# Second layer's input projection written out tile by tile, with its transposes inside it

## The reference, cut to what matters

```
p = x @ w_in                                   # 1024 -> 2888 columns
qc, kc, vc, qd, kd, vd, qi, ki, wi = split_cols(p, ODD_SPLIT)   # 512,512,512,512,128,128,512,64,8
new_rows = (kc, vc, kd, vd, ki)                # returned as caches, token by token
lam = exp(sum(lam_q1*lam_k1)) - exp(sum(lam_q2*lam_k2)) + lam_init
oc = diff_attention(qc, kc_all, vc_all, q_pos, lam, ...)
od = dsa_attention(qd, kd_all, vd_all, qi, ki_all, wi, q_pos)   # indexer picks 256 keys
mix = concatenate([oc, od]) @ w_out
x = layer_norm(ALPHA * x + mix, g1, b1)        # x is the residual
```

## Time and profile before

| | |
|---|---|
| median of 3 runs | 4275.34 us (4273.2 to 4279.86) |
| the profiled execution's own time | 4281.68 us |
| its span, first to last instruction | 4279.9 us |
| TensorE matmul busy | 3564.1 us (83%) |
| DVE busy | 2087.3 us (49%) |
| ACT busy | 910.1 us (21%) |
| mean granted TensorE clock | 0.891 of full speed |

### The profile page before, as it was taken

The page is one execution under the profiler, slowest core; times in us unless marked ns, Lnnn a source line. Parts: engine busy times, 40 slices in busy tenths (PEclk is TensorE's granted clock), DMA queues, the critical chain, the costliest instruction groups (busy, mean ns, idle before and its releaser), DMA issues. The chain is left out here.

```text
span 4279.9 us, 61244 instructions
## 1 busy us (share of the span) xinstructions
PE 3564.1 (83%) x26492; PEld 3237.0 (76%) x26492; DVE 2087.3 (49%) x2944; ACT 910.1 (21%) x1681; POOL 174.7 (4%) x75
## 2 busy tenths in 40 slices
PE   7977379858899999989967777777655989999997
PEld 7977169838899999979964445555434879999996
DVE  3115876565523232451125888988665452323235
ACT  1015311121201010120014444443223020101011
POOL 0010000002200000010020000000000220000001
PEclk9988589978999999989985788887677999999998
DMA  3110000011111111111120000001111111111111
GB/s 101 44 56 5 0 4 4 11 62 35 35 45 42 44 45 45 45 30 44 41 75 1 1 1 1 1 1 30 40 40 21 39 30 45 45 45 43 42 45 47
DMA packets 244527, 142.06 MB, mean 33 GB/s; under 512 B 36101, under 2 KB 237978, under 8 KB 243770
## 3 DMA queue, kind: packets, MB, share of 16 engines
q1 hardware_dynamic: 243320, 138.22, 11.2%
q10 hardware_dynamic: 962, 0.20, 0.0%
HBM read 123.14 MB, written 15.32 MB: 32 GB/s over the span
## 5 line engine op out<-in xcount | busy, mean ns | idle before, releaser
L238 PE MATMUL psum<-rounded,rounded 128*128 128x364 f32 x13536 | 2279.7, 330 | 96.6 <-DVE rounded L668 42.5
L238 PEld LDWEIGHTS psum<-rounded,rounded 128*128 128x128 f32 x13536 | 2270.6, 189 | 106.7 <-issue 81.7
L222 DVE CAST rounded<-arena 128x1024 fp32r<-128x1024 f32 x188 | 134.0, 713 | 401.5 <-PE psum L238 385.5
L541 ACT ACTIVATE arena<-psum 128x1092 f32<-128x1092 f32 x64 | 69.4, 1084 | 1213.7 <-PE psum L238 1213.7
L555 DVE CAST rounded<-arena 128x1092 fp32r<-128x1092 f32 x64 | 46.7, 729 | 533.1 <-ACT arena L544 533.1
L224 DVE TENSOR_TENSOR rounded<-arena,rounded 128x1024 fp32r<-128x1024 f32 x188 | 282.2, 1501 | 6.5
L2034 PE MATMUL psum<-arena 128*128 128x128 f32 (+2 forms) x1424 | 244.8, 327 | 42.2 <-ACT arena L2098 42.0
L1359 PE MATMUL psum<-arena 64*64 64x64 f32 x8160 | 256.7, 220 | 23.9 <-POOL arena L1543 12.5
L1359 PEld LDWEIGHTS psum<-arena 64*64 64x64 f32 x8160 | 246.1, 136 | 35.4 <-DVE arena L1496 18.4
L2034 PEld LDWEIGHTS psum<-arena 128*128 128x128 f32 (+1 forms) x1424 | 220.0, 235 | 67.6 <-issue 41.8
L2018 PE MATMUL psum<-arena 128*128 128x128 f32 (+1 forms) x712 | 143.2, 338 | 133.2 <-ACT arena L2089 132.6
(11 more groups left out here) (228 smaller groups left out, 2749.0 us busy)
## 6 DMA issues: line engine op xcount, KB each, us to landing
arena<-in_w_ff_up SPq DMA_DIRECT2D x128, 256.0 KB, 3.2
arena<-in_w_ff_down SPq DMA_DIRECT2D x128, 256.0 KB, 3.1
arena<-in_w_in_odd SPq DMA_DIRECT2D x46, 256.0 KB, 3.3
arena<-in_w_in_even SPq DMA_DIRECT2D x40, 256.0 KB, 3.3
x_kept<-arena SPq DMA_DIRECT2D x1, 4368.0 KB, 12.4
arena<-x_kept SPq DMA_DIRECT2D x1, 4368.0 KB, 13.1
arena<-in_x_prompt SPq DMA_DIRECT2D x1, 4096.0 KB, 18.7
arena<-in_cache_c_k SPq DMA_DIRECT2D x4, 1024.0 KB, 5.4
```

The lines of the kernel that those rows point to most:

```text
L222: nc.vector.tensor_copy(rounded(m, high), low).then_inc(self.weights_high, 1)
L238: last = nc.tensor.matmul(m.ps[:, out:out + TB], rounded(m, w)[:, k, :], rounded(m, x(k))[:, b * TB:(b + 1) * TB], start=(k == 0 and n == ...
```

## The change

`project_odd` is written out for every engine, with 23 tiles and no loop. The index keys and index weights share one tile (72 columns used), whose keys are copied to the other 64 partitions by a DMA. The order is: index keys, four tiles of C keys, D keys, four of C values, D values, then twelve of queries. While TensorE multiplies tile `u` it transposes tile `u - 2` (of the first eleven) in three groups, ahead of blocks k = 1, 4 and 7, into PSUM banks 3 and 7. DVE moves them out behind the next weight split. Keys go through two staging buffers, stored by SP when it has issued the load of the tile six later. Values are stored in two DMAs of all prompt rows each, and two for the sample.

The norm writes `x` to eight other tiles (`norm.dest`). SP writes them to DRAM (`x_kept`, 4368 KB) when all eight are made, and the setup block of `odd_attention` reads them back into `m.x` behind the three first constants and ahead of the distance table. `turn_rows` and its `join` are gone; lambda is computed in the new block, right behind the norm. Two attention buffers get their own room since `m.p` has 18 tiles instead of 24.

```
+ODD_TILES = ([("idx", 2816, 17)] + [("ck", 512 + 128 * a, 4 + a) for a in range(4)] + [("dk", 2048, 16)]
+             + [("cv", 1024 + 128 * a, 8 + a) for a in range(4)] + [("dv", 2176, 12)]
+             + [("cq", 128 * a, a) for a in range(4)] + [("iq", 2304 + 128 * a, 12 + a) for a in range(4)]
+             + [("dq", 64 * a, 8 + a) for a in range(4)])
 def project_odd(m, norm):
-    linear(m, "in1", 24, loads, 2, [(0, 1), (1, 3), (3, 4), (4, 5), (5, 6)], lambda k: m.x[:, k, :],
-           evacuate, norm=norm)
+    norm.dest = p[:, 8:16, :]
+    groups = [(0, 4), (4, 8), (8, 9)]
+    staged = [p[:, 14 + i, 0:512].rearrange("p (t c) -> p t c", t=4) for i in range(2)]
...
+        def _(sp):
...
+            for u in range(tiles):
+                ring.load(sp, 0, u, True, lambda slot: loads(u, slot))
+                if u == 3:
+                    sp.wait_ge(ring.x_high, ring.operands + 8)
+                    sp.dma_start(io["x_kept"], p[:, 8:16, :].rearrange("p k t -> p (k t)")).then_inc(kept, 16)
+                v = u - 6
+                if v in keys:
+                    store_rows(v)
+                if v == keys[0]:
+                    sp.wait_ge(turned, group_at(v, 2) + 1)
+                    sp.dma_start(p[64:128, 17, :], p[0:64, 17, :]).then_inc(doubled, 16)
+                if v == ODD_TURNED[-1]:
+                    sp.wait_ge(rows, group_at(v, 2) + 1)
+                    store_values("c_v", m.vn)
+                    store_values("d_v", m.vd)
...
+        def _(pe):
+            norm.tensor(pe)
+            def turn(u, g):
+                name, _, tile = ODD_TILES[u]
+                n = group_at(u, g)
+                if n >= 2:
+                    pe.wait_ge(rows, n - 1)
+                pe.wait_ge(ring.freed, ring.tiles + u + 1)
...
+            for u in range(tiles):
+                if u == 1:
+                    norm.scales_read(pe)
+                if u >= 2:
+                    pe.wait_ge(ring.freed, ring.tiles + u - 1)
+                def ready(k):
+                    if u == 0:
+                        pe.wait_ge(ring.x_split, ring.operands + k + 1)
+                    if u - 2 in ODD_TURNED and k in (1, 4, 7):
+                        turn(u - 2, k // 3)
+                ring.multiply(pe, 0, u, lambda k: high[:, k, :], lambda k: m.x[:, k, :], ready)
...
+        def _(act):
+            norm.scalar(act, ring, high)
+            act.wait_ge(lam_p, 2)
+            nc.scalar.activation(m.lam[:, 0:2], m.lam[:, 0:2], ACT.Exp).then_inc(lam_e, 1)
...
+        def _(dve):
+            norm.vector(dve, ring, high, lambda: ring.split(dve, 0, 0, 0, True))
+            def move(u, g):
...
+                    to = stores_before(u, g)
+                    if to >= 2:
+                        dve.wait_ge(stored[to % 2], 16 * (to // 2))
...
+            nc.vector.tensor_tensor(m.lam_in[:, 0:4:2, :], m.lam_in[:, 0:4:2, :], m.lam_in[:, 1:4:2, :], ALU.mult)\
+                .then_inc(lam_p, 1)
+            dve.wait_ge(lam_p, 1)
+            nc.vector.tensor_reduce(m.lam[:, 0:2], m.lam_in[:, 0:4:2, :], AX.X, ALU.add).then_inc(lam_p, 1)
+            for u in range(1, tiles):
+                ring.split(dve, 0, 0, u, True)
+                if u == 2:
...
+                    dve.wait_ge(kept, 16)
+                if u - 3 in ODD_TURNED:
+                    for g in range(len(groups)):
+                        move(u - 3, g)
 class Norm:
-            nc.scalar.activation(m.x[:, k, :], m.x[:, k, :], ACT.Identity, scale=m.col(self.gain + k),
+            nc.scalar.activation(self.dest[:, k, :], m.x[:, k, :], ACT.Identity, scale=m.col(self.gain + k),
-                nc.scalar.activation(rounded(m, high[:, k, :]), m.x[:, k, :], ACT.Copy).then_inc(ring.x_high, 1)
+                nc.scalar.activation(rounded(m, high[:, k, :]), self.dest[:, k, :], ACT.Copy).then_inc(ring.x_high, 1)
-            tt(rounded(m, m.x[:, k, :]), m.x[:, k, :], rounded(m, high[:, k, :]), ALU.subtract)\
+            tt(rounded(m, m.x[:, k, :]), self.dest[:, k, :], rounded(m, high[:, k, :]), ALU.subtract)\
-def turn_rows(m):
...
 def odd_attention(m):
-    spare = p[:, 8:12, :].rearrange("p k t -> p (k t)")
+    spare = room(4 * T)
-    index = p[:, 22:24, :].rearrange("p k t -> p (k t)")
+    index = room(2 * T)
...
             sp.dma_start(on[:, 0, 0:128], c[:, CONST["corner"][0]:CONST["corner"][0] + 128]).then_inc(dist_loaded, 16)
+            sp.dma_start(m.arena[:, m.x_at:m.x_at + 8 * T], io["x_kept"]).then_inc(x_back, 16)
             sp.wait_ge(free, 1)
             sp.dma_start(probs, c[:, CONST["distS"][0]:CONST["distS"][0] + LS]).then_inc(dist_loaded, 16)
 def build(nc, io):
     project_odd(m, norm)
-    turn_rows(m)
     odd_attention(m)
```

More of the change, by code:

```diff
@@ L192, in __init__ @@
         self.x_high, self.x_split = nc.alloc_semaphore("operand_high"), nc.alloc_semaphore("operand_split")
-        self.next = (0, 0, 0, 0)
+        self.next = (0, [0] * SLOTS, 0, 0)
     def begin(self, at, ndma, pieces, tiles):
@@ L199, in begin @@
         self.ndma = ndma
-        self.next = (self.pieces + pieces, self.loads + pieces // SLOTS * ndma * 16,
+        self.next = (self.pieces + pieces,
+                     [n + len(range(s, pieces, SLOTS)) * ndma * 16 for s, n in enumerate(self.loads)],
                      self.operands + 8, self.tiles + tiles)
@@ L217, in split @@
         low, high = self.low[:, u % SLOTS], self.high[:, u % HIGHS]
-        dve.wait_ge(self.loaded[u % SLOTS], fills * 16 * self.ndma + (self.loads + (u // SLOTS + 1) * 16 * self.ndma))
+        dve.wait_ge(self.loaded[u % SLOTS], fills * 16 * self.ndma + (self.loads[u % SLOTS] + (u // SLOTS + 1) * 16 * self.ndma))
         if not first or u >= HIGHS:
@@ L601, in __init__ @@
         self.source = m.x if source is None else source
+        self.dest, self.totals = m.x, (m.sum, m.square_sum)
         self.P = Steps(nc, f"{name}_pe", ["mean", "sums", "rstd"])
@@ L616, in tensor @@
         for b in range(NB):
-            last = nc.tensor.matmul(m.ps[:, b * 512:b * 512 + TB], m.c("mean"), m.sum[:, b * TB:(b + 1) * TB],
+            last = nc.tensor.matmul(m.ps[:, b * 512:b * 512 + TB], m.c("mean"), self.totals[0][:, b * TB:(b + 1) * TB],
                                     start=True, stop=True)
         last.then_inc(*self.P.step("mean"))
-        for v, total in enumerate((m.sum, m.square_sum)):
+        for v, total in enumerate(self.totals):
             for t, (b, o) in enumerate(self.spots):
@@ L1691, in _ @@
             affine(3)
-def turn_rows(m):
[L1698 to L1800, removed]
-                sp.wait_ge(A.sem, A.done(t, "k"))
-                sp.wait_ge(V.sem, V.done(t, "rest"))
-                for name, src in (("c_k", rows[0:n, t % 2, 0:512]), ("c_v", m.vn[0:n, t, :]),
-                                  ("d_k", rows[0:n, t % 2, 512:640]), ("d_v", m.vd[0:n, t, :]),
-                                  ("d_kidx", rows[0:n, t % 2, 640:704])):
-                    sp.dma_start(out(name), src).then_inc(stored[t % 2], 16)
-            sp.wait_ge(stored[0], 16 * 5 * 5)
-            sp.wait_ge(stored[1], 16 * 5 * 4)
@@ L2215, in index_scalar @@
             for h, half in enumerate((slice(0, 64), slice(64, 128))):
-                last = nc.scalar.activation(qi_s[half, :, half], p[half, 16:20, t.cols], ACT.Copy)
+                last = nc.scalar.activation(qi_s[half, :, half], p[half, 12:16, t.cols], ACT.Copy)
         else:
@@ L2219, in index_scalar @@
                 act.wait_ge(index_made, t.base)
-            nc.scalar.activation(qi[0:64, 0:4, 0:t.n], p[0:64, 16:20, t.cols], ACT.Copy)
-            last = nc.scalar.activation(qi[64:128, 4:8, 0:t.n], p[64:128, 16:20, t.cols], ACT.Copy)
+            nc.scalar.activation(qi[0:64, 0:4, 0:t.n], p[0:64, 12:16, t.cols], ACT.Copy)
+            last = nc.scalar.activation(qi[64:128, 4:8, 0:t.n], p[64:128, 12:16, t.cols], ACT.Copy)
         last.then_inc(index_q, 1)
@@ L2570, in build @@
     norm = Norm(m, "ln1", ROWS["ffng"], ROWS["ffnb"], m.acc)
-    m.p = m.arena[:, after_x:after_x + 24 * T].rearrange("p (k t) -> p k t", k=24)
-    m.work = after_x + 24 * T
-    m.ring = m.work
+    m.p = m.arena[:, after_x:after_x + 18 * T].rearrange("p (k t) -> p k t", k=18)
+    m.work = after_x + 18 * T + (9 * 640 + 72)
+    m.ring = m.odd_work = m.work
     assert m.ring + RING <= columns - 8 * T
     project_odd(m, norm)
-    turn_rows(m)
     odd_attention(m)
```

134 lines of the change are left out of this document (112 added, 22 removed).

## The result

Measured side by side, the changed kernel takes 4268.11 us (median of 12 runs, 4258.68 to 4274.38) and the kernel before 4275.43 us (12 runs, 4271.44 to 4282.21). The ratio is 0.998, 95% interval 0.9971 to 0.9989: 7.3 us faster, where 18.5 were forecast. The profiled execution of the changed kernel took 4258.68 us, the lowest of its runs, while the one of before (4281.68) was near the highest of its. So the two profiles are compared stage by stage and not by their ends.

The account below looks back on a forecast made before the run. TensorE was taken to set the projection's pace, with nothing overlapping it in the 45.6 us before attention. Terms -12.0 - 30.8 + 16.7 + 0.6 + 7.0 = -18.5 us took 4275.34 to 4257 us, range 4243 to 4271.

Parts of the forecast that it names:

- one tile less: Second layer's projection: 24 to 23 tiles at TensorE's pace of 11.97 us each, -12.0 us.
- `turn_rows` goes: Block between projection and attention setup: removed, so setup starts 1.5 us after the last matmul, -30.8 us.
- transposes in the tiles: Projection: 99 transposes at 0.135 us (13.4) and 33 interruptions at 0.1 (3.3) between products, together +16.7 us.
- lambda: Between the norm's end and the second tile's split: two small DVE operations, 0.3 us each, +0.6 us.
- x ahead of the table: Attention's setup block: 4368 KB of x queued before the distance table delay its cast, +7.0 us.
- norm to attention: From the norm's first matmul to the attention's first: 366.2 us today, should be 348; all terms sum to -18.5 us.
- Attention and everything behind it: Attention and later stages: same instructions on other addresses, cold start as before; zero, 4 us either way.
- Loops and straight code: Projection: 23 tiles ran without a visible gap across loop turns, so writing them out gains nothing.
- Rival (c): Projection: clock falls behind each transposed group, +43 us, total 4300; deciding from 0.56 cold blocks per group; 0.10 with similar stalls.
- rival (a): Setup block: the queue doesn't delay the distance table, the +7.0 falls away, 4250; chance 0.12 together with cheap transposes.
- Rival (d): Projection: chain of stores and moves slower; stores landing 3 us later than 2.1 make TensorE wait, 4259; no chance given.

Follow-up runs that it names:

- control: The changed kernel run once more with nothing edited: 4267.69 us, ratio 0.9978 to the kernel before.
- nine instructions: The changed kernel with 9 more satisfied TensorE waits in diff_finish, moving the second MLP's loop head 9 instructions on: 4256.84 us, ratio 0.9956.
- The kernel before with its padding: The kernel before with 121 more satisfied TensorE wait instructions between attention and MLP, its loop head at 89 modulo 256: 4287.22 us, ratio 1.0024.

## Why the prediction was wrong

The steps of the changed stage held in kind, and their sum came out better than forecast:

| step | forecast | measured |
|---|---|---|
| one tile less | -12.0 | -12.0 (2177.45 - 2165.45) |
| `turn_rows` goes | -30.8 | -30.9 (evacuation to setup 1.34, was 32.20) |
| transposes in the tiles | +16.7 | +10.9 (11 x 0.99) |
| lambda | +0.6 | +0.5 |
| x ahead of the table | +7.0 | +8.3 (18.57 - 10.24) |
| norm to attention | -18.5 | -23.2; by the stage -22.6 (343.5 with nine instructions, where the norm is a long one as before) |
| attention | 0, 4 either way | +1.7 between the two profiles, of which +2.1 is lasting and the rest scatter |
| turns of the MLP's loop | 0 | +9.6 |

By the stage, the lasting part of the attention and the turns this makes -10.9 us. The medians differ by 7.3, with an interval of 4.7 to 12.4 (9.5 beside the control); so what is left is within the scatter, of which the norms are one source.

**The step that failed** is "Attention and everything behind it run the same instructions on other addresses ... Zero". For the MLP, the other address of TensorE's own instructions was the cost. "Loops and straight code: ... writing them out gains nothing" was right for the stage itself and asked only for a gain. It did not ask what 2200 more instructions do to the loops behind. No rival had it either. The reading under it was of another kind of loop: the projection's four tiles are 586 instructions, and in the kernel before the queue has no "q8 instruction" packet from 1994 to 2185 us while that loop turns. It needed no page, and the MLP's loop of 2333 needs some at each turn. That the changed kernel's head came to lie within eight instructions of a page's end was chance, as was the good place in the kernel before. With the head moved by nine instructions the kernel is 20.1 us faster than the one before, and with 135 it is 19.5, where 18.5 was forecast. That this agrees so well is partly luck: the cheaper transposes (-5.8) stand against x (+1.3) and the attention (+2.1), and the rest is within the scatter. Rival (c)'s "0.56 cold blocks per group" divides the wrong figure (24 / 43); the sum turns at 18.5 / 43 = 0.43. Nothing hung on it.

The Trainium skill ("Runtime: NRT & Kernel Launch", section "Instruction fetch mechanics") says that each engine fetches its instructions sequentially in 16 KB pages on a DMA queue of its own, and that a taken branch to a page that isn't held stalls until it is fetched. The runs agree, and they add what the page does not say: TensorE stood idle 0.5 to 1.1 us at the turn with the head at the four other places tried, and 3.6 to 5.1 us in the changed kernel, whose head has no product left in its page. It would have named the risk. It could not have given the number, and a count of the new program alone does not tell where in it a page ends.

**Transposes.** The term was mis-sized. 0.135 us each came from a row in which only transposes run; between products one costs 0.11. The 0.1 per interruption was taken as half of an idle weight load, and nothing of it was seen. Rival (c) fell: the clock stayed at 1.00 through all tiles with transposes, and also with twice as many. The Trainium skill's rule ("TensorE: Matmul & The Clock Gate", Part 4: PE-mode transpose), by which the full clock does not engage for transposes, did no harm here, at 9 or 18 among 72 products. These tiles are mostly products, so they don't test the rule itself; the row against it is that of `turn_rows`.

**x.** The queue delayed the table by the price in bytes and 1.3 us more; rival (a) fell. **Stores.** Rival (d)'s premise came true in part, 3.7 us instead of 2.1, and cost nothing, since the slack of 2.7 us was larger than the 1.6 us. DVE waits longer only because it arrives early.

**Attention.** Between the two profiles it is -3.0 us in the prompt part, +2.1 in the first sample part and +2.6 in the second. Only the 2.1 is lasting: the first sample part takes 118.0 us in both profiles of the old kernel, padded or not, and 120.0 to 120.2 in all eight of the changed one and its versions. The prompt part goes from 682.2 to 688.7 among those eight, and the second sample part took 266.9 and 270.0 in the two of the old kernel. Most of the 2.1 can be seen. The same 40 matmuls, by stretch, before and after:
```profile
2924.03:2938.84 14.81, 14.80 (x40) 7.02 (x40) 10.37 (x18) 9.43 (x19) 0.00 (x0) 1.00 0.00 1
```
```profile
2890.78:2907.17 16.39, 16.39 (x40) 7.66 (x40) 10.37 (x18) 9.43 (x19) 0.00 (x0) 0.90 0.00 1
```
They start in the changed kernel before the clock is back at its full level, 1.6 us. The kernel before with its padding has 14.81 again, and the eight profiles of the changed one and its versions have 16.4 to 16.5, so it goes with the program and not with the execution. Why the clock rises later there is open: all padding stood behind the attention, and none ahead of it was tried.

## What to carry to other kernels

A change that makes an engine's program longer or shorter moves every loop behind it. After such a change compare the gaps at the loop turns of the stages that were not touched, and if one has grown, move the loop head by a few instructions before judging the change. Look at the packets of the instruction queue at that time: they tell this stall from any other. When two single profiles are compared, first take out the stages whose clock differs by chance, as the norms' did here. A transfer that nobody waits for goes behind the one that somebody does, on the same queue. Short transposes between long products cost their own time and no more.

## What the runs showed of the hardware

- A turn of TensorE's loop of 16 tiles (2333 instructions) leaves it idle 0.5 to 1.1 us at the four good places tried. The earlier projection's loop of four tiles (586 instructions) turned without a gap (275.52 busy of 275.53) and without a packet on the instruction queue.
- With the loop head within eight instructions of the end of a 16 KB page, the idle time is 3.6 to 5.1 us in the changed kernel, and the clock falls to its lower level behind it (0.68 over 5 us, 0.63 over 7). With that the turn costs 5.3 to 6.6 us.
- TensorE went on 1.3 to 1.8 us after the page it waited for had landed, in every gap of this kind.
- 99 further transposes in float32 between products (eight of 128x128 and a smaller one in each tile) took 0.11 us each.
- 36 small matmuls of a norm took 7.68 us or 4.6 to 5.0, at a clock of 0.50 or 0.80 to 0.88, in executions of the same instructions.
- Stores of 256 KB in rows of 512 bytes landed in 3.7 us; the same bytes in `turn_rows`, in rows of 2048 bytes, took 2.1. Whether the row length or the weight loads beside them made the difference is not shown.
